# Router logits between the output pieces, expert weights in long rows, and the gather and its branch rearranged in a two-block transformer kernel

## The reference, cut to what matters

```python
x = x + gt1[:, None, :] * (o @ w_out[l])                 # output projection of the attention, 2048 x 2048
h = modulate(rms_norm(x, g_ffn[l]), sh2, sc2)            # rms_norm(x) * g_ffn * (1 + sc2) + sh2
...
g_logits = (t @ w_rg + b_rg)                             # t is h; 4 groups: the best one
e_logits = (t @ w_re + b_re).reshape(n_tok, 4, 8)        # 32 experts: the best two of that group
...
for e in range(N_EXPERTS):                               # 32
    a = jax.nn.silu(t @ w_gate[e]) * (t @ w_up[e])       # 2048 x 512 each
    y = y + combine[:, e:e + 1] * (a @ w_down[e])        # 512 x 2048
x = x + gt2[:, None, :] * y
```

## Time and profile before

| | |
|---|---|
| time, median of 3 runs (lowest to highest) | 2445.85 us (2441.64 to 2447.97) |
| the profiled execution: its time | 2444.84 us |
| the profiled execution: span, first to last instruction | 2442.7 us |
| mean granted clock of TensorE | 0.977 of full speed |
| busy: PE, PEld, DVE, ACT, POOL | 2222.4, 1639.7, 1388.2, 732.9, 43.0 us |
| moved by DMA | 761.77 MB, 312 GB/s on average |

### The profile page before, as it was taken

One profiled execution on the slowest core, in us unless ns is written; L12 is line 12 of the kernel. 1 busy time (PEld: TensorE's weight loads), 2 busy tenths in 40 slices (PEclk: granted clock), 3 DMA queues, 4 the chain that ended last, 5 costly groups with the idle time before them and its releaser, 6 DMA issues. The chain is left out here.

```text
span 2442.7 us, 37024 instructions
## 1 busy us (share of the span) xinstructions
PE 2222.4 (91%) x14593; PEld 1639.7 (67%) x14593; DVE 1388.2 (57%) x2051; ACT 732.9 (30%) x1343; POOL 43.0 (2%) x61
## 2 busy tenths in 40 slices
PE   6999999999999989979999978998888888888886
PEld 5899988788899888778898864444444444444442
DVE  6877788887787888666454634333333333333334
ACT  5444444454435434356554422000000000000001
POOL 0100000000000000030000000000000000000000
PEclk9999999999999999989999979999999999999998
DMA  8877766788777567674344256999999999999997
GB/s 320 322 298 292 275 242 247 307 314 338 293 295 274 224 260 265 246 269 148 147 141 152 105 227 245 422 422 422 422 422 422 422 422 422 422 422 422 422 422 322
DMA packets 108686, 761.77 MB, mean 312 GB/s; under 512 B 12288, under 2 KB 15392, under 8 KB 16800
## 3 DMA queue, kind: packets, MB, share of 16 engines
q1 hardware_dynamic: 108432, 759.49, 78.3%
q10 hardware_dynamic: 144, 0.79, 0.1%
HBM read 757.28 MB, written 2.95 MB: 311 GB/s over the span
## 5 line engine op out<-in xcount | busy, mean ns | idle before, releaser
L2312 PE MATMUL b_ps<-s_raw,s_window 128*64 128x256 f32 x4096 | 461.2, 382 | 58.2 <-DVE x_tokens L2538 39.3
L2312 PEld LDWEIGHTS b_ps<-s_raw,s_window 128*64 128x64 f32 x4096 | 295.6, 137 | 235.4 <-issue 72.6
L1175 DVE TENSOR_TENSOR s_w_tail<-s_raw,s_w_head 128x1024 fp32r<-128x1024 f32 x292 | 344.9, 1223 | 39.1 <-ACT s_w_head L778 39.0
L947 PE MATMUL b_ps<-s_h_head,s_w_head 128*128 128x256 f32 x1184 | 346.1, 292 | 0.0
L948 PE MATMUL b_ps<-s_h_tail,s_w_head 128*128 128x256 f32 x1184 | 339.1, 286 | 0.0
L949 PE MATMUL b_ps<-s_h_head,s_w_tail 128*128 128x256 f32 x1184 | 338.7, 286 | 0.0
L778 ACT ACTIVATE s_w_head<-s_raw 128x1024 fp32r<-128x1024 f32 x292 | 293.0, 1049 | 102.3 <-DMA s_raw<-in_w 70.6
L1262 DVE SCALAR_TENSOR_TENSOR s_ada_acc<-s_raw,s_c_col,s_ada_acc 128x2048 f32<-128x2048 f32 x120 | 282.3, 2352 | 0.0
L2332 PE MATMUL b_ps<-s_raw,s_diag 128*64 128x512 f32 x1024 | 237.8, 600 | 39.2 <-DMA s_raw<-in_w_down 24.0
L947 PEld LDWEIGHTS b_ps<-s_h_head,s_w_head 128*128 128x128 f32 x1184 | 231.1, 195 | 12.9 <-issue 9.4
L948 PEld LDWEIGHTS b_ps<-s_h_tail,s_w_head 128*128 128x128 f32 x1184 | 231.3, 195 | 0.2
(11 more groups left out here) (336 smaller groups left out, 3147.8 us busy)
## 6 DMA issues: line engine op xcount, KB each, us to landing
s_raw<-in_w SPq DMA_DIRECT2D x198, 1024.0 KB, 5.1
s_raw<-in_w_ada SPq DMA_DIRECT2D x128, 1024.0 KB, 5.2
s_raw<-in_w_gate SPq DMA_DIRECT2D x128, 1024.0 KB, 24.1
s_raw<-in_w_up SPq DMA_DIRECT2D x128, 1024.0 KB, 26.5
s_raw<-in_w_down SPq DMA_DIRECT2D x128, 1024.0 KB, 26.5
x_tokens<-in_x SPq DMA_DIRECT2D x1, 2048.0 KB, 7.8
s_rel<-in_rel SPq DMA_DIRECT2D x1, 2048.0 KB, 11.6
s_raw<-mod_rows SPq DMA_DIRECT2D x2, 1024.0 KB, 12.3
```

The source lines that it names most:

```text
L947: pe.matmul(out, head, m_head, start=first, stop=False, skip_group_check=True)
L1175: dve.tensor_tensor(w_tail[:, g % SPLITS, cols], raw[:, slot["w", g], cols], w_head[:, g % SPLITS, cols].bitcast(F32), ALU.subtract)\
L2312: ins = pe.matmul(psum[64 * h:64 * h + 64, c // 4, 0:T], window[:, 4 * (c % 4) + k, :], raw[:, c, k * 512 + h * T:k * 512 + h * T + T], st ...
```

## The change

**Logits.** Steps "turn_x" and "logits" are added to the list of `second_attention`: after output piece (1, 2) PE turns the four feature tiles of block 0 of x (8 transposes; ACT and DVE copy them out into `h_t`), after (1, 3) it makes the logits of these four (4 products: 36 columns of the router's weights stationary, 256 tokens moving, accumulating in one bank); the same for block 1 after (2, 0) and (2, 1), for block 2 after (3, 0) and (3, 1), and for block 3 at the end. There the logits are copied, turned back (2 transposes), and scaled by 1/rms and given their constant in 4 DVE operations. This is possible on x itself since gain goes into the router's weights and shift into a constant: three DVE operations over 128x576 and one of 16 columns ("router_weights", after piece kb 3), one small PE product and one DVE addition ("router_shift"). The operands come in one load of 427 KB ("late") that SP issues between raw loads, once `c2` and `slope_bias`, whose place it takes, are read; `h_t` takes the place of `rel`.

**experts.** Norm, turn and logits at its start are gone, and POOL's 1/rms is made in `second_attention`. ACT makes the head of x in two operations over 128x2048, DVE the tail in eight over 128x512, of which two stand before the gather and six within it. The gather is otherwise the same. PE's usual loop is now the first branch, right behind the gather; the copy of the first window stands ahead of DVE's branch.

**Weights.** Per expert 4 loads instead of 12: gate and up 4 MB each (128 rows of 32 KB), down 2 MB twice (rows of 16 KB; its array is stored with all 32 KB of a partition together). PE waits once per load, and gives back a place as large as the load (`PIECES_E = 4`). `x_head` and `x_tail` lie where `down` lies later, so for the first expert only gate and up are loaded at the start, and down when the gather is through.

```diff
+TURNS_2 = {(1, 2): [("turn_x", 0)], (1, 3): [("logits", 0)], (2, 0): [("turn_x", 1)], (2, 1): [("logits", 1)],
+           (3, 0): [("turn_x", 2)], (3, 1): [("logits", 2)]}
...
+    return [("norm",)] + steps + [("turn_x", 3), ("logits", 3), ("logit_turn",), ("x_rstd",)]
...
+            if pieces[i][2:] == ("feat", "kb", 2):
+                sp.wait_ge(sem["shifted"], at("shifted", ("A", 7, 1)))
+                sp.wait_ge(sem["bias"], 1)
+                sp.dma_start(early[:, 0:N_LATE], d["late"]).then_inc(sem["router_in"], 16)
...
+            elif kind == "turn_x":
+                n = s[1]
+                for t in range(TT):
+                    pe.wait_ge(sem["x_added"], at("x_added", (n, t)))
+                for j in range(2):
+                    ps = bank_for(pe, ("turn_x", n, j))
+                    for k in range(2):
+                        for t in range(TT):
+                            col = k * T + t * P
+                            ins = pe.transpose(ps[:, col:col + P], x_tiles[:, t, 4 * n + 2 * j + k, :], ident)
+                    ins.then_inc(full_sem(("turn_x", n, j)), 1)
...
+                for k in range(4 * n, 4 * n + 4):
+                    ins = pe.matmul(ps[0:36, 0:T], w_r[:, k, :], h_t[:, k, :], start=k == 0, stop=k == KT - 1)
...
-    raw = sb("raw", [P, PIECES_E, CHUNK_ELEMS])
+    raw = sb("raw", [P, 8, CHUNK_ELEMS])
+    with ExitStack() as passing:
+        x_head, x_tail = (passing.enter_context(nc.sbuf_tensor(f"s3_{name}", [P, TT, D], F32R))
+                          for name in ("x_head", "x_tail"))
+    down = sb("down", [P, FT, CHUNK_ELEMS])
...
-        if c < 8:
-            src = (w_gate if c < 4 else w_up)[pick_e, :, (c % 4) * CHUNK_ELEMS:(c % 4 + 1) * CHUNK_ELEMS]
-            src = src.rearrange("a p n -> (a p) n")
+        if c < 2:
+            src = (w_gate, w_up)[c][pick_e, :, :].rearrange("a p n -> (a p) n")
+            dst = raw[:, 4 * c:4 * c + 4, :].rearrange("p c n -> p (c n)")
         else:
-            src = w_down[pick_e, c - 8, :, :].rearrange("a p n -> (a p) n")
-        sp.dma_start(raw[:, c, :], src).then_inc(arrived[c], 16)
+            src = w_down[pick_e, :, 2 * (c - 2) * D:2 * (c - 1) * D].rearrange("a p n -> (a p) n")
+            dst = down[:, 2 * (c - 2):2 * (c - 1), :].rearrange("p c n -> p (c n)")
+        sp.dma_start(dst, src).then_inc(arrived[c], 16)
...
-        for c in range(PIECES_E):
+        for c in range(2):
+            load_expert_piece(sp, 0, c)
+        sp.wait_ge(sem["gathered"], KT)
+        for c in range(2, PIECES_E):
             load_expert_piece(sp, 0, c)
...
+        few = most_tokens(pe) <= CROWD
         pe.wait_ge(sem["picks"], 1)
         for k in range(KT):
+            if k % 4 == 0:
+                pe.wait_ge(sem["x_tail"], TT * (k // 4 + 1))
...
-        with pe.If(crowded(pe)):
+        with pe.If(few):
+            with pe.Fori(0, EXPERTS) as e:
+                pe.wait_ge(sem["window"], e + 1)
+                for c in range(8):
+                    if c % 4 == 0:
+                        pe.wait_ge(arrived[c // 4], e * 16 + 16)
...
+                    if c % 4 == 3:
+                        ins.then_inc(sem["used"], 1)
...
+                for m_ in range(FT):
+                    if m_ % 2 == 0:
+                        pe.wait_ge(arrived[2 + m_ // 2], e * 16 + 16)
...
+        many = crowded(dve)
+        for m in range(1, KT, 2):
+            if m in TAIL_AT:
+                for t in range(TT):
+                    x_tails(t, TAIL_AT[m])
+            dve.wait_ge(sem["gathered"], m + 1)
+            dve.tensor_scalar(picked[:, m, 0:PICKED], psum[:, m % 4, :], gain[:, m:m + 1],
+                              shift[:, m:m + 1], ALU.mult, ALU.add).then_inc(sem["read_v"], 1)
...
+        dve.tensor_copy(window[:, :, :], picked[:, :, 0:WINDOW]).then_inc(sem["window"], 1)
+        with dve.If(many):
```

More of the change, by code:

```diff
@@ L1429, in followers @@
                 out.append((i + 3, ("onorm", name)))
+        if piece[:2] == ("feat", "kb") and piece[2] == 3:
+            out += [(i, ("router_weights",)), (i + 2, ("router_shift",))]
+        if piece[:1] == ("out",):
+            out += [(i, s) for s in TURNS_2.get(piece[1:], ())]
         return out
@@ L1484, in second_attention @@
             take(s, 7)
+        elif kind == "router_shift":
+            take(s, 6)
+        elif kind == "turn_x":
+            for j in range(2):
+                take(("turn_x", s[1], j), 4 + j)
+        elif kind == "logits" and s[1] == 0:
+            take(("logits",), 6)
+        elif kind == "logit_turn":
+            take(s, 7)
     for i in range(n_pieces):
@@ L1645, in _ @@
         ins.then_inc(sem["bias"], 1)
+        pool.wait_ge(sem["x_squared"], 1)
+        over_rms(pool, chain, ssq_x, ssq_pair[:, :, :], ssq[:, 2:4], half[:, 2:4], shared["rstd3"][:, :])\
+            .then_inc(sem["rstd"], 1)
     @block.scalar
@@ L2093, in experts @@
     rows = raw_flat[:, 4 * D:8 * D].rearrange("p (a n) -> p a n", a=4)
[L2094 removed]
+    scratch = down
     w_gate, w_up, w_down = d["w_gate"], d["w_up"], d["w_down"]
@@ L2188, in squares @@
             return act.activation(scratch[:, t, cols], x[:, t, cols], ACT.Square, accum_out=ssq_x[:, t, n:n + 1])
-        act.wait_ge(sem["rstd"], 1)
-        for k in range(X_SPLITS):
-            x_heads(k)
+        for t in range(TT):
+            act.activation(x_head[:, t, :], x[:, t, :], ACT.Copy, scale=rstd3[:, t:t + 1]).then_inc(sem["x_head"], 1)
         act.wait_ge(sem["exp_in"], 1)
@@ L2286, in _ @@
+        with pe.Else():
+            pe.wait_ge(sem["dense_h"], 1)
+            for t in range(TT):
+                ins = pe.matmul(psum[:, 6, t * P:(t + 1) * P], ones, diag[:, t, :], start=True, stop=True)
+            ins.then_inc(sem["dense_row"], 1)
+            pe.wait_ge(sem["dense_h"], 2)
             with pe.Fori(0, EXPERTS) as e:
@@ L2427, in _ @@
                                           in1=r[:, 10, sl], op0=ALU.mult, op1=ALU.add))
-        for k in range(X_SPLITS):
-            x_tails(k)
+        x_tails(0, 0)
         dve.wait_ge(sem["sums"], 1)
@@ L2643, in build @@
             turned = first_block(nc, ctx, part, d, x, ssq_x, c0, mod)
+        shared = {name: ctx.enter_context(nc.sbuf_tensor(name, shape, F32))
+                  for name, shape in (("h_t", [P, KT, T]), ("logit", [P, 2, 64]), ("early", [P, 4 * T]), ("rstd3", [P, TT]),
+                                      ("gain3", [P, KT]), ("sconst", [P, 36]))}
         with ExitStack() as part:
-            second_attention(nc, ctx, part, d, x, ssq_x, c0, mod, mod_dram, turned)
+            second_attention(nc, ctx, part, d, x, ssq_x, c0, mod, mod_dram, turned, shared)
         with ExitStack() as part:
-            experts(nc, ctx, part, d, x, ssq_x, c0, mod, mod_dram, out)
+            experts(nc, ctx, part, d, x, ssq_x, c0, mod, mod_dram, out, shared)
```

377 lines of the change are left out of this document (186 added, 191 removed).

## The result

The changed kernel takes 2412.86 us, median of four runs (2410.86 to 2413.75), against 2445.83 before: a ratio of 0.9866 (0.9849 to 0.9883), 33 us less, with 2417 predicted and 2407 to 2436 as the range. The profiled execution has 2410.86 us and a span of 2409.1, against 2442.7.

A forecast was written before the change was run, and what follows sets the result against it. PE bounds the output projection, the weight stream the expert loop, with the prologue paid in full; -15.5 (gather end) - 9.5 (stream start) + (921.0 - 928.5) + 4.0 = -28.5 gives 2416.3 us profiled, 2417 median, range 2407 to 2436.

The forecast's parts named there:

- PE between output pieces: Output projection: three times 8 transposes (1.12 us) and 4 products (0.88 us) lengthen it by 7.0 us, at most 8.
- Rival D: Output pieces: logits don't leave the path, gain falls by 8 us to 2425; worse case of main line, no own chance.
- x to first comparison: From x complete to routing's first comparison: last turn, logits and small operations take 5.8 us, before 25.57.
- Comparison to pick: Routing, first comparison to pick: 14.3 us, before 14.43, with DVE 0.6 us late waiting for ACT.
- Gather: 64 passes after pick: 14 at the lower clock in 5.9 us, 50 at 0.235 us, together 17.6 us.
- G': End of the gather in the changed kernel: predicted at 1463.5 us, 15.5 us earlier than before.
- To the first load: After the gather: first expert's down issued 0.1 us later, second's gate at 8.8 us, no hole in the stream.
- The worth of the branch order: Entry to PE's expert loop: with the 3.8 us stand still there, the stream's hole would be 1 us.
- The stream: Expert weight loads: 8.7 ns fixed per row, 29.26 us per expert with long rows, 921.0 us in all.
- Coarse release: Expert loop: releasing whole loads doesn't starve the queue; PE's cycle of 30.2 us is absorbed by up's landing, cost 0.
- Rival B: Expert loop: PE becomes the bound, 0.9 us per expert adds up, 29 us come back, 2446; chance 0.06.
- Behind the last byte: Last expert: its distribution begins 5.85 us after the last byte, before 1.9, adding 4.0 us.

The follow-up runs named there:

- late12: Changed kernel with logits 1 and 2 moved to the end, ahead of turn 3, the turns left between output pieces; 2413.16 us (0.9866).
- all_end: Changed kernel with all turns and logits at the end of the attention program, none between output pieces; 2416.55 us (0.9889).
- b_long: Kernel before with only the weights part: four long loads per expert, waits and release as coarse as the change's; 2432.68 us (0.9957).
- branch: Changed kernel with the dense variant first in PE's code again, the usual loop behind it; 2422.17 us (0.9911).
- rows8_one: Changed kernel with its four loads per expert, but weights stored so that a row is 8 KB; 2430.74 us (0.9944).
- fine: Changed kernel with 8 KB rows in twelve loads per expert, waited for and given back one by one; 2431.88 us (0.9941).

## Why the prediction was right, and where its terms were off

**What bounds the kernel.** Right. The end moved with the start of the stream, its rate, and what follows its last byte, and PE's work between the output pieces was paid in full.

**PE between output pieces: +7.0 predicted, +9.0 measured.** This is the term of the sum that was mis-sized, and it lay outside its own bounds of 6 to 8. The transposes were right: 1.04 to 1.06 us for eight, with 1.12 predicted. The logits were not. Four products in eight passes were put at 0.11 us each, from the earlier trace rows, that is 0.88. They take 8 x 0.215 = 1.7, 1.89 with the draining (in the timeline above), and late12 shows that a logits step costs 2.1 us there. Three of them are 6.3; the 2.7 that are left are 0.9 for each turn. router_shift stands further ahead and costs next to nothing: with everything else at the end (all_end) x is complete after 383.9 us, before after 383.7. The rate of 0.11 belongs to products that have 64 stationary columns and come in pairs, one for each half of the result's partitions. That a product with 36 columns alone has no partner is the likely reason, which no run tested; a product with 128 stationary columns takes the same time. The row to take was this one of the kernel before, whose passes of 256 columns start (3.62 - 0.38) / 15 = 0.216 us apart:

```profile
1341.37 3.62 PE L1877 MATMUL b_ps<-s_squares,c_sb 128*128 128x256 f32 x16
```

Rival D (over 10) did not come.

**x to first comparison: 5.8 predicted, 5.82 measured.** The sum was right by two errors: the logits took 0.7 to 0.9 more, while copies of 512 columns took 0.60 on ACT and 0.69 on DVE and not 0.81, and the handovers less.

**Comparison to pick: 14.3 against 14.14.** Right, and the 0.6 us for ACT came up as well. The timeline of DVE in the kernel after:

```profile
1434.80 0.16 DVE L2463 TENSOR_REDUCE s_rs<-s_r 128x2 f32<-128x8 f32 x1 [0.63 <-ACT s_r L2280]
```

**Gather: 17.6 against 16.3, G' 1463.5 against 1460.0.** Mechanism right, size off by the clock. The prediction let 14 passes run at the lower clock, as before; in the kernel after there are eight, until 1446.87. This is 6 x 0.2 = 1.2 us, nearly the whole difference; why the clock came back earlier in the gather stays open. The rest of the 3.5 comes from the first block (-4.1), the logits (+2.0) and the routing (-0.2).

**To the first load: 0.1 predicted, 0.05 measured**, and gate of the second expert came 9.1 us behind G' where 8.8 was predicted. The DMA share of 0.98 over the first 24 us shows that no hole opened. The worth of the branch order was named as 1 us and is 7. The stand of PE was taken as 3.8 from before and measured 5.7 in the changed code; the low clock behind such a stand, 2 us, was not counted; and down was to cover 3.2 us of the delay (12 - 8.8) and covered 1.3 (7.6 later, 6.3 without transfer).

**The stream: 921.0 predicted, 917.3 measured.** Per expert 29.26 predicted, 29.22 measured; the rest is latency and ramp, 4.1 predicted, under 2 measured. The last byte is read from the stretches at the end of the kernel after:

```profile
2376.00:2377.00 1.00, 1.00 (x11) 0.47 (x8) 0.01 (x1) 0.00 (x0) 0.00 (x0) 1.00 1.04 442
2377.00:2378.00 1.00, 0.75 (x4) 0.28 (x4) 0.60 (x2) 0.53 (x2) 0.00 (x0) 1.00 0.39 164
```

The rate breaks off at about 2377.4, and 394.3 MB in 917.3 us are 430 GB/s. The price of a row was the boldest step of the prediction, two points of a line with one of them a lone stretch of 4 us. It held: 8.7 ns predicted, 9.2 and 10.0 measured between other lengths, and in the DMA records of the kernel after a row of 32 KB takes 1215 ns and one of 16 KB 613 (medians), where 1216.4 and 612.5 were predicted. By the HBM limit per core of 358 GB/s (the Trainium skill, DMA: Bandwidth & Descriptors, Specifications) the 394.3 MB would take 1101 us, an estimate from that figure, and not the 938.4 that the prediction put beside it. It didn't bind here, on one core alone: the traces have 431, 422 and 410. The same table of the Trainium skill gives 435 GB/s as the fabric ceiling; the long rows come within 1% of it, so by that figure still longer ones have next to nothing left to bring.

**Coarse release: 0 predicted, 0 measured** (the DMA share is 1.00), but the reason was partly wrong. PE's cycle was put at 30.2 us, 0.9 more than the stream. It is 27.5: that is how far apart the first four experts start, when gate and up are already there (ACT's activation at 1468.99, 1496.47, 1523.92, 1551.38). The prediction had counted the 9.73 us of up's transfer in it, beside which PE does the 7.03 of gate. Without them the parts that it names add up to 7.03 + 7.03 + 1.4 + 7.09 + 4.9 = 27.5. Rival B, which needed the 0.9 to add up, had no ground, and deserved less than its 0.06.

**Behind the last byte: +4.0 predicted.** L2395 begins 8.0 us after 2377.4, not 5.85, and 6.1 later than the 1.9 of before. Up landed 7.6 us before the last byte and not 9.8, so PE's 15.6 us reach further past it. Here the wait was right and its size was not. Stream and end together are off by -1.5.

**The sum.** G' came 3.5 us earlier, stream and its end were 1.5 shorter, the last stretch 0.1 longer: 2416.3 - 4.9 = 2411.4, against 2410.86 measured; 0.3 of the rest is that time and span differ by 1.8 us here and by 2.1 before. Without the first block's -4.1, which no step could know, the steps miss by 1.3. That is so little because +2.0 for the logits stands against -3.0 in routing, gather and stream, which is luck. Two of its signs failed for the same reasons: the output pieces grew by 9 us and not by 6 to 8, and L2395 of the last expert came 8.0 us after the last landing and not 5.9. G' at 1460.05, outside its 1461 to 1466, is the first block's.

## What to carry to other kernels

When a stream of weights bounds a stage, price a transfer by its rows: rate at two row lengths gives a fixed time per row (here 9 to 10 ns), and storing the weights so that a row is 16 to 32 KB is worth 2% of the stream over 8 KB, however many loads carry them. Waits and releases may then be as coarse as the load as long as the engine's own cycle is shorter than the transfer; only the last load pays. Look at what stands between the last wait and the first product of such a stage: a PE that waits for nothing shown, here at the entry of a far branch, gives its first place back later by as much as it stands and by what the lower clock behind it adds (5.5 and 2 us here), and the load behind that place comes late. And take the duration of a product from a row with the same use of the array, not from one with the same number of columns moving.

## What the runs showed of the hardware that was not expected

- The body of a branch that stands right behind it is entered in 0.13 us; the one behind the other body in 3.8 us (kernel before), 4.1 (b_long) and 5.7 (branch), without anything in the profile that PE waits for.
- Two products of 64 stationary columns side by side take 0.11 us per pass of 256 columns each, a single one of 36 columns 0.215, as one of 128 does.
- The rate of a stream goes 431, 422, 410 GB/s for rows of 16 to 32, 8 and 4 KB, at a DMA share of 1.00 to 1.03 each time.
- Loads in one queue don't land in strict order of bytes: of the last expert, up was complete 7.6 us before the last byte, although 4 MB stood behind it, which take 9.8.
- The granted clock falls to 0.50 for a spell in every third or fourth expert of rows8_one, behind a wait of PE, and not at all in the loop of fine, which has the same rows, the same rate and shorter waits for loads (0.6 us at most against 2.1, from 1900 to 2000).
- The same code has more spells at the lower clock in some executions than in others, worth 2.3 us here, and its first block varies by 5.6 us.
